# Groups of eight tokens instead of four in the one-hot products that build the experts' weights

## The reference, cut to what matters

```python
def peer_ffn(h, w_q, sub_keys, u_tab, v_tab):
    ...
        v_half, i_half = lax.top_k(sc, PEER_TOPK_HALF)
        cand = (v_half[:, :, 0, :, None] + v_half[:, :, 1, None, :]).reshape(t, PEER_HEADS, -1)
        ...
        top_s, pos = lax.top_k(cand, PEER_TOPK)
        expert = jnp.take_along_axis(cand_idx, pos, axis=-1)
        g = jax.nn.softmax(top_s, axis=-1)
        u = u_tab[expert]
        act = jax.nn.gelu(jnp.einsum('thkd,td->thk', u, xc).astype(jnp.float32), approximate=False)
        w = (g * act).astype(xc.dtype)
        return jnp.einsum('thk,thkd->td', w, v_tab[expert])
```

## Time and profile before

| what | us |
|---|---|
| three runs | 2659.93, 2660.98, 2662.16 |
| median of the runs | 2660.98 |
| profiled execution, first to last instruction (span) | 2658.2 |
| profiled execution's own device time | not listed beside its span |
| PE busy | 2496.3 (94%) |
| DVE busy | 1593.1 (60%) |
| ACT busy | 1035.6 (39%) |
| U stage of layer 0 with groups (rounds 9 to 15) | 887 to 1086 |
| V stage of layer 0 with groups (rounds 0 to 6) | 1086 to 1297 |
| the same stages of layer 1 | 2034 to 2232, 2232 to 2442 |

### The profile page before, as it was taken

The page is one execution under the profiler, slowest core; times in us unless marked ns, Lnnn a source line. Parts: engine busy times, 40 slices in busy tenths (PEclk is TensorE's granted clock), DMA queues, the critical chain, the costliest instruction groups (busy, mean ns, idle before and its releaser), DMA issues. The chain is left out here.

```text
span 2658.2 us, 49516 instructions
## 1 busy us (share of the span) xinstructions
PE 2496.3 (94%) x18422; PEld 2253.2 (85%) x18422; DVE 1593.1 (60%) x3479; ACT 1035.6 (39%) x1519; POOL 0.2 (0%) x4
## 2 busy tenths in 40 slices
PE   6999869789999999999999889988999999999997
PEld 6998744448999999999999645578999999999997
DVE  4785421620998677788655223207995777887554
ACT  4564110321555544334444212114555443334443
POOL 0000000000000000000000000000000000000000
PEclk9999989679999999999999896789999999999999
DMA  5454133121455444444555330024555444445553
GB/s 199 185 189 158 64 121 127 58 79 64 166 166 189 151 150 151 141 144 154 178 182 181 127 150 32 32 80 145 173 185 163 149 151 143 143 155 169 182 181 111
DMA packets 83203, 376.63 MB, mean 142 GB/s; under 512 B 9484, under 2 KB 9612, under 8 KB 76464
## 3 DMA queue, kind: packets, MB, share of 16 engines
q1 hardware_dynamic: 83120, 375.58, 40.9%
HBM read 374.49 MB, written 1.05 MB: 141 GB/s over the span
## 5 line engine op out<-in xcount | busy, mean ns | idle before, releaser
L294 PE MATMUL bank<-h_lo,tile_hi 128*128 128x256 f32 x2560 | 722.7, 282 | 0.0
L293 PE MATMUL bank<-h_hi,tile_hi 128*128 128x256 f32 x2048 | 592.2, 289 | 19.1 <-DVE tile_lo L1846 13.9
L293 PE MATMUL bank<-hidden_hi,tile_hi 128*128 128x256 f32 x2048 | 590.1, 288 | 7.1 <-DVE hidden_lo L2060 7.1
L294 PE MATMUL bank<-hidden_lo,tile_hi 128*128 128x256 f32 x2048 | 580.6, 284 | 0.0
L295 PE MATMUL bank<-hidden_hi,tile_lo 128*128 128x256 f32 x2048 | 580.3, 283 | 0.0
L295 PE MATMUL bank<-h_hi,tile_lo 128*128 128x256 f32 x2048 | 579.9, 283 | 0.0
L294 PEld LDWEIGHTS bank<-h_lo,tile_hi 128*128 128x128 f32 x2560 | 491.5, 192 | 0.0
L2028 ACT ACTIVATE tile_hi<-wbuf 128x1024 fp32r<-128x1024 f32 x256 | 271.2, 1059 | 448.0 <-PE bank L295 443.6
L2057 DVE TENSOR_TENSOR tile_lo<-wbuf,tile_hi 128x1024 fp32r<-128x1024 f32 x256 | 312.6, 1221 | 181.0 <-ACT tile_hi L2028 180.8
L293 PEld LDWEIGHTS bank<-h_hi,tile_hi 128*128 128x128 f32 x2048 | 395.7, 193 | 23.5 <-issue 19.0
L293 PEld LDWEIGHTS bank<-hidden_hi,tile_hi 128*128 128x128 f32 x2048 | 396.1, 193 | 7.4 <-DVE tile_lo L2057 7.4
(11 more groups left out here) (335 smaller groups left out, 2889.7 us busy)
## 6 DMA issues: line engine op xcount, KB each, us to landing
wbuf<-in_peer_u SPq DMA_DIRECT2D x256, 512.0 KB, 3.2
wbuf<-in_peer_v SPq DMA_DIRECT2D x256, 512.0 KB, 3.2
wbuf<-in_w_in SPq DMA_DIRECT2D x16, 2048.0 KB, 7.8
wbuf<-in_peer_q SPq DMA_DIRECT2D x8, 2048.0 KB, 7.4
wbuf<-in_hyb_in SPq DMA_DIRECT2D x6, 1928.0 KB, 7.0
wbuf<-in_mla_in SPq DMA_DIRECT2D x3, 1536.0 KB, 9.4
wbuf<-in_mla_uq SPq DMA_DIRECT2D x3, 1536.0 KB, 6.3
wbuf<-in_w_v SPq DMA_DIRECT2D x2, 2048.0 KB, 7.3
```

The source lines that it names most:

```text
L293: nc.tensor.matmul(out, hi[:, cols], other_hi, start=start, stop=False, **kw)
L294: nc.tensor.matmul(out, hi[:, cols], other_lo, start=False, stop=False, **kw)
```

## The change

GROUP becomes 8. A stage has 32 groups of sixteen products instead of 64 groups of eight. The one-hot tensors and `wide` get twice as large (from 6 KB to 12 KB of each partition in all) and the entries that a product reads lie 16 bytes apart. The dynamic-DMA scratch becomes 1024 bytes, set explicitly where the default stood. The table of groups is written anew: six per round in the first two rounds (none behind tiles 2 and 5), four per round, behind the even tiles, in the other five: 2 x 6 + 5 x 4 = 32. The last group of a stage now stands behind tile 6 of its round, and the condition that leaves out the one-hots behind it names the group instead of the tile.

```diff
-    GROUP = 4
+    GROUP = 8
...
-        MANY, ROUNDS_MANY, WEIGHING = 10, 4, 7
+        MANY, ROUNDS_MANY, WEIGHING = 6, 2, 7
 
         def groups_behind(q, j, many):
-            first = MANY * q if many else MANY * ROUNDS_MANY + STEP * (q - ROUNDS_MANY)
-            at_ = ([0], [1], [2], [3, 4], [5], [6], [7], [8, 9])[j] if many else [j]
+            first = MANY * q if many else MANY * ROUNDS_MANY + STEP // 2 * (q - ROUNDS_MANY)
+            at_ = ([0], [1], [], [2], [3], [], [4], [5])[j] if many else ([0], [], [1], [], [2], [], [3], [])[j]
             return [(first + n, n % 2) for n in at_]
...
-                            if not (last and j == STEP - 1):
+                            if not (last and n == NGROUP - 1):
                                 one_hots(dve, 0, n + 1, 1 - b, first_done[0], hots_done[0])
                             weigh(dve, 0, n, b, weights_done[0], weighted[0])
...
-    nc = bacc.Bacc("TRN2", target_bir_lowering=False, num_devices=1)
+    nc = bacc.Bacc("TRN2", target_bir_lowering=False, num_devices=1, dynamic_dma_scratch_size=1024)
```

## The result

The changed kernel takes 2772.18 us (median of 4 runs, 2770.95 to 2774.60) against 2661.57 us of the kernel before beside it: a ratio of 1.0417, 95% interval 1.0403 to 1.0432. It is 110.6 us slower. The prediction's number was 2765.8 us, its range 2654 to 2786 us. The number came out close; the reason given for it did not, as the experiments show.

A forecast was written before the change was run, and what follows sets the result against it. TensorE was taken as the bound, by the distances between its products' starts. Groups -3.7, change of stages -0.7 and the step +109.2 sum to +104.8 us, on the median 2660.98 giving 2765.8 us; range 2654 to 2786.

The forecast's parts named there:

- The bound: TensorE, busy 94% of the span; time in its stages is the sum of distances between its products' starts.
- Fewer, longer groups, -3.7 us: TensorE's one-hot products: 128 groups of sixteen take 134.4 us instead of 138.1; may be -2 to -6.
- the change of stages, -0.7 us: U to V stage: last group's weighing ends earlier, gelu is late next; gap 0.33 us shorter in two layers.
- VectorE and the scratch at nothing: DVE's larger one-hot instructions stay hidden behind TensorE; the scratch only shifts tensor addresses; both cost nothing.
- The step, +109.2 us: `hot_second` read at 16 bytes instead of 8: 53.3 ns of each of 2048 products doubles, other 9 ns stay; chance 0.52.
- the bounds: Cost of the step: nothing at one entry per cycle, or +128 us if the whole distance is bytes passed.
- rival 1: The step between entries that a product reads costs nothing, leaving -4.4 us: 2656.6 us; chance 0.36.
- rival 2: The step costs another amount: half the term gives 2711 us, upper bound, whole 62.5 ns doubled, 2784.6; chance 0.10.
- The signs that the prediction named for itself: Sixteen products some 1.9 us, tiles with group 4.8 us apart, longer L1710 wait, 4.0 us at stage change, starts 115 ns apart.
- rival 3 (VectorE): VectorE becomes the bound, its larger float16 instructions falling to the float32 rate: +15 us, 2671 us; chance 0.02.

The follow-up runs named there:

- experiment 8: Changed kernel with `hot_first` in quarters of two tokens (moving step 4 bytes) and `hot_second` in halves of four (8 bytes): 2603.28 us, ratio 0.978.
- Experiment 2: Changed kernel with groups of eight and its table, but both one-hot tensors kept in halves of four tokens (step 8 bytes): 2656.07 us, ratio 0.998.
- experiment 1: Kernel before with only the dynamic-DMA scratch set to 1024 bytes: 2662.08 us, ratio 1.0003.
- experiment 3: Also written `second_16b`: kernel before with small scratch, `hot_second` (stationary) padded to a 16-byte step, `hot_first` (moving) left at 8: 2666.60 us, ratio 1.0022.
- experiment 4: Kernel before with small scratch, `hot_first` (moving) padded to a 16-byte step, `hot_second` (stationary) left at 8: 2764.76 us, ratio 1.0391.
- experiment 10: As experiment 8 (moving step 4 bytes), but `hot_second` (stationary) in the changed kernel's layout, step 16 bytes: 2657.58 us, ratio 0.9985.
- experiment 7: Kernel before with small scratch, groups of four, `hot_first` in pieces of two tokens (moving step 4 bytes), made by two instructions: 2611.85 us, ratio 0.9813.
- experiment 9: As experiment 8, but `hot_first` dense per token (moving step 2 bytes): 2640.78 us, ratio 0.9921 against the kernel before.

## Why the prediction was right or wrong

**The bound: right.** TensorE's stages are the sum of its starts. The account by starts closes to 0.3 us for the changed kernel (by the spans) and for experiment 8 (by the medians), closer than the rounding of its rows would let one expect.

**Fewer, longer groups, -3.7 us, and the change of stages, -0.7 us: right.** Experiment 2 has both without the rest: -5.05 us, an interval of -2.9 to -7.7 us by its ratio. The gap went from 4.35 to 4.00 us in both layers. What the prediction called late next, the gelu, is late next.

**VectorE and the scratch at nothing: right.** The three distances that can be read came out at 0.34, 0.60 and 0.60 us where 0.33 and 0.60 were forecast; experiment 1 shows the scratch at 1.0003. (Two groups of four are 2 x 1.20 = 2.40 us of VectorE by the earlier trace rows, not 2.42; nothing hangs on it.)

**The step, +109.2 us: right in sign and nearly in size, wrong in mechanism.** It measured 252.2 - 134.4 = 117.8 us. What failed is the choice of the operand: the term gives 53.3 of the 62.5 ns to the load of the stationary operand, doubles them and gives the moving columns nothing. No run shows the 53.3 ns, nor the one entry per cycle that the bounds and the chance of rival 1 name; in their place experiment 8 shows the load's 128 entries within 34 ns, 3.8 per ns, and the moving read accounts for the 62 ns of the kernel before: 32 pieces of 16 bytes at theory E's 1.8 ns are 58. No row of the kernel before told the two operands apart. Experiments 3 and 4 did: 65 ns with the stationary step alone, 118 with the moving one. That the size came out was luck: the moving read, too, touches twice as many pieces at 16 bytes. It was a little low, 1.90 us for sixteen products against 1.97: not 53.3 of the 62.5 ns double but practically all (62 to 118 with the moving step alone). The stationary step adds to it: the changed kernel is 115.7 us over experiment 2, experiment 4 only 103.6 us over the kernel before. The other 12 us come with the stationary step, as 122 ns instead of 118 between products and 138 instead of some 106 ns for the first distance of a group, by the starts of single products. For the distance alone, the upper bound of rival 2 (125 ns) was nearer to 122 than the forecast (115.8).

The signs that the prediction named for itself came out, at or near the sizes it gave: 1.97 us for sixteen products, 4.85 us from group to group, a longer wait at L1710 (1.12 us instead of 0.66), 4.00 us at the change of stages, and no TensorE waiting for the one-hots. All of them ask only how far apart the products are, not which operand sets the distance, so both readings pass.

**Rival 1 (no cost)** is out by the result, **rival 3 (VectorE)** by the rows above. Rival 2 (another amount) is the nearest to what came, by its upper bound. The loads run beside the products: in experiment 8 a load's record is 117 ns and the products are 34 ns apart. In experiment 3 the moving read takes 62 ns and the load some 60 (experiment 10), and together they take 65. So the two don't add, and which of them is the longer has to be asked of each layout.

**What the mistake hid.** Had the moving read been seen as the bound, the same profile would have pointed to the gain of experiment 8: the kernel before already paid 62 ns where 34 do.

## What to carry to other kernels

When several tokens share a tensor with the token innermost, a matmul reads it with a step, and both operands can pay for the 16-byte pieces they touch (the moving one measured at six steps, 34 to 118 ns; the stationary one at two, 34 and 63 ns). Keep small groups innermost (two float16 entries here for the moving operand, four for the stationary one), and weigh that against what the engine that writes the layout pays. When a distance between products fits one operand's arithmetic, compute the other operand's too, and change one layout at a time before believing either.

## What the runs showed of the hardware that was not expected

- The moving read of a float16 product with 64 columns costs about 1.8 ns per 16-byte piece touched: 34, 62, 89, 118 ns for 16, 32, 48, 64 pieces, and 118 ns again when the 64 pieces lie 32 bytes apart. With 8 pieces it is still 34 ns, so something else binds there; what, no run shows.
- The tiles' products move 256 x 4 = 1024 dense bytes, also 64 pieces, and stand 120 ns apart, near the 118 ns of 64 pieces in a one-hot product. Whether the same read bounds them was not tried.
- The load of 128 float16 entries fits in 34 ns at a step of 8 bytes (64 pieces) and takes about 60 ns at 16 bytes (128 pieces). As an estimate from that one distance it is 0.5 ns per piece, a quarter of the moving read's price. Its record, 117 to 119 ns against 166 to 168, is longer than the distance it allows.
- VectorE's `hot_first` over 512 float16 elements took 0.42 us where it reads `is_first` densely and in runs of four 16 bytes apart (experiment 2), 0.625 in runs of two 16 bytes apart, 1.10 when it gathered single elements 16 bytes apart. The length of the runs alone is not the cause: experiment 7 has runs of two as well, 8 bytes apart in `is_first`, and took 0.284 us for 256 elements, as long as the dense `is_first` instruction over 256 (0.29). What goes with the time is how many elements it takes from one 16-byte piece of `is_first`: eight in the earlier trace rows and four in experiments 2 and 7 cost the same, two in experiment 8 and one in experiment 9 cost more. No run varied that alone.
- `second_16b` is 5.5 us over the kernel before, although 222 groups on the path at 0.04 us are 9 us, and its stages with groups are 10.6 us longer by the starts of the same tile products. In its profile stages that no edit touched are shorter, by 2 to 3 us each at two places, in the second attention layer and at layer 1's start (windows of 45.7 and 83.0 us where the kernel before has 47.6 and 85.7, at a slightly higher granted clock). What moves them from one program to the next was not looked into; it is the size of error that a difference in medians carries here.
